# A two-layer attention, scan and expert step on one core: longer runs for the gate and up weights, and a first norm taken tile by tile

## What is computed

```
def adaln(x, g, shift, scale):
    return rms_norm(x, g) * (1 + scale) + shift        # eps 1e-6 inside the root

# attention, layer 0: per head
q = rms_norm(q.reshape(b, t, 16, 64), q_g); k = rms_norm(k.reshape(b, t, 4, 64), k_g)

# experts, after each mixer (t: 640 x 1024)
scores = sigmoid(t @ router_w)                         # 1024 x 16, shared by both layers
...                                                    # one group of 4, then 2 experts in it
hg = einsum('td,edf->tef', t, w_gate)                  # w_gate, w_up: 16 x 1024 x 256
hu = einsum('td,edf->tef', t, w_up)
out = einsum('tef,efd->td', silu(hg) * hu * gates, w_down)   # w_down: 16 x 256 x 1024
```

## Time and profile before

| | |
|---|---|
| runs | 1648.84, 1651.23, 1654.79 us |
| the profiled execution's own time | 1647.64 us |
| its span, first to last instruction | 1645.7 us |
| PE busy | 1452.9 us, 88% of the span |
| DVE, ACT, POOL busy | 581.2, 560.2, 177.6 us |
| bytes moved | 323.25 MB, mean 196 GB/s |
| gate, up, down loads | 40 each, 1 MB each, 20 per layer |

### The profile page before, as it was taken

One profiled execution on the slowest core, in us unless ns is written; L12 is line 12 of the kernel. 1 busy time (PEld: TensorE's weight loads), 2 busy tenths in 40 slices (PEclk: granted clock), 3 DMA queues, 4 the chain that ended last, 5 costly groups with the idle time before them and its releaser, 6 DMA issues.

```text
span 1645.7 us, 18690 instructions
## 1 busy us (share of the span) xinstructions
PE 1452.9 (88%) x7371; PEld 727.6 (44%) x7371; DVE 581.2 (35%) x927; ACT 560.2 (34%) x1228; POOL 177.6 (11%) x177
## 2 busy tenths in 40 slices
PE   5998799999969998488899899899889997899970
PEld 3444454444443333165455455455454444433320
DVE  1133556662450000173545545545452033300004
ACT  4112444441112221253573573573570011122211
POOL 0122000000010000200310400400410100200002
PEclk9999999999979999769999999999999999899985
DMA  9502666469289999633133133133054123999985
GB/s 346 207 1 94 227 198 227 158 206 360 89 307 345 380 379 380 246 107 119 58 121 103 64 116 102 65 114 103 26 187 184 43 73 111 362 368 381 384 311 204
DMA packets 193889, 323.25 MB, mean 196 GB/s; under 512 B 8822, under 2 KB 120006, under 8 KB 193798
## 3 DMA queue, kind: packets, MB, share of 16 engines
q1 hardware_dynamic: 172956, 260.33, 46.5%
q0 software_dynamic: 8496, 31.17, 5.0%
q10 hardware_dynamic: 12352, 30.58, 4.7%
HBM read 279.05 MB, written 42.99 MB: 196 GB/s over the span
## 4 chain that ended last, share of the span: by engine, by line
PE 76%; DVE 9%; DMA 6%; ACT 4%; issue 3%; SPq 2%; POOL 0%; ACTq 0%; DVEq 0%; POOLq 0%
PE ps L945 10%; PE ps L1041 10%; PE ps L1201 8%; PE ps L1096 8%; PE ps L732 7%; PE ps L966 5%; PE ps L895 4%; PE ps L679 3%; PE ps L1043 2%; PE ps L822 2%; PE ps L806 2%; DMA mem<-in_expert_w_up 2%; PE ps L1180 2%; PE ps L929 1%; PE ps L1172 1%
## 5 line engine op out<-in xcount | busy, mean ns | idle before, releaser
L945 PE MATMUL ps<-mem 128*32 128x512 f32 (+1 forms) x1408 | 204.2, 606 | 9.3 <-DMA mem<-in_expert_w_up 7.2
L1041 PE MATMUL ps<-mem 128*128 128x512 f32 x384 | 171.2, 599 | 0.2 <-ACT mem L1566 0.2
L1201 PE MATMUL ps<-mem 128*128 128x512 f32 x320 | 139.0, 593 | 3.2 <-issue 2.7
L1096 PE MATMUL ps<-mem 128*128 128x512 f32 x320 | 140.7, 593 | 0.3 <-ACT mem L1566 0.3
L1891 DVE TENSOR_TENSOR mem<-ps,mem 128x256 f32<-128x256 f32 x28 | 11.9, 425 | 362.1 <-ACT mem L1386 362.1
L1961 DVE SCALAR_TENSOR_TENSOR mem<-mem 128x642 f32<-128x642 f32 x96 | 92.6, 965 | 87.5 <-ACT mem L1490 85.0
L945 PEld LDWEIGHTS ps<-mem 128*32 128x32 f32 (+1 forms) x1408 | 60.3, 119 | 136.5 <-issue 134.0
L966 PE MATMUL ps<-mem 128*32 128x512 f32 (+1 forms) x704 | 106.5, 609 | 11.8 <-DMA mem<-in_expert_w_down 8.0
L732 PE MATMUL ps<-mem 128*128 128x512 f32 x240 | 109.2, 613 | 1.9 <-DVE mem L1665 1.9
L1041 PEld LDWEIGHTS ps<-mem 128*128 128x128 f32 x384 | 72.0, 192 | 82.3 <-issue 81.5
L1526 ACT ACTIVATE mem<-mem,small 128x128 f32<-128x128 f32 x320 | 95.2, 392 | 25.4 <-DMA mem<-cum_rows 25.4
(11 more groups left out here) (315 smaller groups left out, 1944.5 us busy)
## 6 DMA issues: line engine op xcount, KB each, us to landing
mem<-in_mod_w SPq DMA_DIRECT2D x24, 2048.0 KB, 8.6
mem<-in_expert_w_gate SPq DMA_DIRECT2D x40, 1024.0 KB, 12.5
mem<-in_expert_w_up SPq DMA_DIRECT2D x40, 1024.0 KB, 14.1
mem<-in_expert_w_down SPq DMA_DIRECT2D x40, 1024.0 KB, 12.9
mem<-cum_rows SPq DMA_DIRECT2D x40, 512.0 KB, 5.3
slot_rows<-mem ACTq DMA_DIRECT2D x28, 512.0 KB, 7.0
mem<-slot_rows ACTq DMA_DIRECT2D x26, 512.0 KB, 8.1
slot_rows<-mem SPq DMA_DIRECT2D x1, 12288.0 KB, 53.6
```

The source lines that it names most:

```text
L945: last = nc.tensor.matmul(ps[c:c + w, 2 + j, :], XGT[j][:, k, c:c + w], GUW[l][m][:, k, :], start=(k == 0), stop=(k == KD - 1))
L1041: nc.tensor.matmul(ps[:, b, :], w[:, k, :], HT[:, k, SEQ:TOK], start=(k == 0), stop=(k == KD - 1))
L1096: last = nc.tensor.matmul(ps[:, ZBANK[t], :], HT[:, k, t * P:(t + 1) * P], WZ[2 * k // KD][:, k % (KD // 2), :], start=(k == 0), stop=(k = ...
L1201: last = nc.tensor.matmul(ps[:, 4 + n % 4, :], YT[b][:, k, t * P:(t + 1) * P], w[:, k, :], start=(b == 0 and k == 0), stop=(b == 1 and k = ...
```

## The change

Four edits, in one program.

1. **Gate and up weights.** Both are read as `e (p k) f`: partition p holds the rows 8p to 8p+7, which lie together in memory, one run of 2048 floats (8 KB) for each partition and transfer. The tile becomes `[p, 2, k, f]`: all of gate, then all of up. The product takes `GUW[l][m][:, :, k, :]`, two pieces of 256 columns. Since row 8q+k of the weights is now on partition q of step k, the tokens' columns are permuted in the same way: `norm_row` writes its first result into the scratch `JUNK`, and the addition of the shift writes element `8q+k` to column `128k+q` of `H`. The router's weights are loaded in the same order. The down weights are as before.
2. **First norm.** `X` comes as three transfers on three semaphores (context tile; latent tiles 1 and 2; tiles 3 and 4). ACT takes square and root of each tile in turn, with the copies of turned tiles between them, and takes one root of a dummy before, which loads the function table. DVE takes a reciprocal and scales, tile by tile. PE turns all five tiles ahead of `early_chunk(0)`.
3. **Head norm.** The multiplication by 1/64 and the addition of eps move into ACT's root.
4. Semaphores are shared between uses to stay within their number; a wait on `s_h` guards `JUNK` in `norm_row` (from the second tile on) and in the attention's residual.

```diff
-        GUW = [[page(at, 4 * PG).rearrange("p (k n) -> p k n", k=KD) for at in order] for order in (...)]
+        GUW = [[page(at, 4 * PG).rearrange("p (a k n) -> p a k n", a=2, k=KD) for at in order] for order in (...)]
...
-            sp.dma_start(X[:, 0, :], x_prompt[0]).then_inc(s_x, 16)
-            sp.dma_start(X[:, 1:NT, :], x_sample[0].rearrange("(t p) n -> p t n", p=P)).then_inc(s_x, 16)
+            sp.dma_start(X[:, 0, :], x_prompt[0]).then_inc(s_xy, 16)
+            sp.dma_start(X[:, 1:3, :], xv[:, 0:2]).then_inc(s_rows, 16)
+            sp.dma_start(X[:, 3:NT, :], xv[:, 2:NT - 1]).then_inc(s_x, 16)
...
-            sp.dma_start(RW[:, 0:KD, :], router_w.rearrange("(k p) e -> p k e", p=P)).then_inc(s_x, 16)
+            sp.dma_start(RW[:, 0:KD, :], router_w.rearrange("(p k) e -> p k e", p=P)).then_inc(s_x, 16)
...
-                gv = w_gate[l].rearrange("e (k p) f -> e p k f", p=P)
-                uv = w_up[l].rearrange("e (k p) f -> e p k f", p=P)
+                gv = w_gate[l].rearrange("e (p k) f -> e p (k f)", p=P)
+                uv = w_up[l].rearrange("e (p k) f -> e p (k f)", p=P)
...
-                    sp.dma_start(GUW[l][m][:, :, 0:FF], gv[e]).then_inc(pk["lgu"][m], 16)
-                    sp.dma_start(GUW[l][m][:, :, FF:2 * FF], uv[e]).then_inc(pk["lgu"][m], 16)
+                    sp.dma_start(GUW[l][m][:, 0].rearrange("p k f -> p (k f)"), gv[e]).then_inc(pk["lgu"][m], 16)
+                    sp.dma_start(GUW[l][m][:, 1].rearrange("p k f -> p (k f)"), uv[e]).then_inc(pk["lgu"][m], 16)
...
-            early_chunk(0)
             norm_transposes(0)
+            early_chunk(0)
             early_chunk(1)
...
-                            last = nc.tensor.matmul(ps[c:c + w, 2 + j, :], XGT[j][:, k, c:c + w], GUW[l][m][:, k, :],
+                            last = nc.tensor.matmul(ps[c:c + w, 2 + j, :], XGT[j][:, k, c:c + w], GUW[l][m][:, :, k, :],
...
+            order(nc.scalar.activation(ssq[:, 5:6], eps[:, :], ACT.Sqrt))
+            for t in range(NT + 2):
+                if t < NT:
+                    row_lengths(t)
+                if t >= 2:
+                    norm_columns(t - 2)
...
-                nc.scalar.activation(rs[:, :], rs[:, :], ACT.Sqrt).then_inc(s_sdq, 1)
+                nc.scalar.activation(rs[:, :], rs[:, :], ACT.Sqrt, scale=1.0 / HD, bias=eps[:, :]).then_inc(s_sdq, 1)
...
-                order(nc.vector.scalar_tensor_tensor(H[:, t, :], X[:, t, :], ssq[:, t:t + 1], MB[1][:, 1, min(t, 1), :],
+                if t >= 1:
+                    dve.wait_ge(s_h, nn * NT + t)
+                order(nc.vector.scalar_tensor_tensor(JUNK, X[:, t, :], ssq[:, t:t + 1], MB[1][:, 1, min(t, 1), :],
                                                      op0=ALU.mult, op1=ALU.mult))
-                nc.vector.tensor_tensor(H[:, t, :], H[:, t, :], MB[1][:, 0, min(t, 1), :], ALU.add).then_inc(s_h, 1)
+                nc.vector.tensor_tensor(H[:, t, :].rearrange("p (k q) -> p q k", k=KD), JUNK.rearrange("p (q k) -> p q k", k=KD),
+                                        MB[1][:, 0, min(t, 1), :].rearrange("p (q k) -> p q k", k=KD), ALU.add).then_inc(s_h, 1)
...
-                nc.vector.tensor_scalar(rs[:, :], rs[:, :], 1.0 / HD, EPS, ALU.mult, ALU.add).then_inc(s_varq, 1)
```

More of the change, by code:

```diff
@@ L230, in backbone @@
         HELD = [len(range(m, NE, RING)) for m in range(RING)]
-        GUW = [[page(at, 4 * PG).rearrange("p (k n) -> p k n", k=KD) for at in order] for order in ((18, 22, 10, 14, 28), (22, 10, 18, 14, 28))]
+        GUW = [[page(at, 4 * PG).rearrange("p (a k n) -> p a k n", a=2, k=KD) for at in order] for order in ((18, 22, 10, 14, 28), (22, 10, 18, 14, 28))]
         WD = [page(at, 2 * D).rearrange("p (k n) -> p k n", k=2) for at in (26, 5, 7, 36, 34)]
@@ L310, in backbone @@
         s_gqk = sem("s_gqk")
-        s_qkv, s_sq, s_v, s_varq, s_sdq, s_qn, s_qg, s_t2, s_qf, s_tq, s_tqe = (
-            sem(n) for n in "s_qkv s_sq s_v s_varq s_sdq s_qn s_qg s_t2 s_qf s_tq s_tqe".split())
+        s_qkv, s_sq, s_v, s_rsq, s_sdq, s_qn, s_qg, s_t2, s_qf, s_tq, s_tqe = (
+            sem(n) for n in "s_qkv s_sq s_v s_rsq s_sdq s_qn s_qg s_t2 s_qf s_tq s_tqe".split())
         s_S, s_Sc, s_max, s_exp, s_T, s_ptd, s_pta, s_pv, s_oev, s_rx, s_rs, s_Scc = (
@@ L316, in backbone @@
         o_u, o_cv, o_pv, o_y = sem("o_u"), sem("o_cv"), sem("o_pv"), sem("o_y")
-        s_zero, s_clear = sem("s_zero"), sem("s_clear")
+        s_zero, s_rows = sem("s_zero"), sem("s_rows")
         s_ssdin, s_pre_pe, s_pre_act, s_pre_dve = (sem(n) for n in "s_ssdin s_pre_pe s_pre_act s_pre_dve".split())
@@ L595, in _ @@
                 sp.wait_ge(ES["x2"], NT + t + 1)
-                sp.dma_start(y_prompt[0] if t == 0 else y_sample[0, (t - 1) * P:t * P, :], X[:, t, :]).then_inc(s_yout, 16)
+                sp.dma_start(y_prompt[0] if t == 0 else y_sample[0, (t - 1) * P:t * P, :], X[:, t, :]).then_inc(s_xy, 16)
         @block.tensor
@@ L629, in logit_columns @@
                 if t == 0:
-                    pe.wait_ge(s_x, 64)
+                    pe.wait_ge(s_x, 48)
                     if l == 0:
@@ L708, in early_chunk @@
                 mod_chunk(EX[n % 2], n, 7, s_exused[n % 2])
+            norm_transposes(0)
             early_chunk(0)
-            norm_transposes(0)
             early_chunk(1)
@@ L1228, in _, with row_lengths, norm_columns @@
             order = Order(act, o_act)
[L1230 to L1243, removed]
+            def row_lengths(t):
+                if t <= 1:
+                    act.wait_ge((s_xy, s_rows)[t], 16)
+                elif t == 3:
+                    act.wait_ge(s_x, 16)
+                order(nc.scalar.activation(SQX, X[:, t, :], ACT.Square, accum_out=ssq[:, t:t + 1]))
+                nc.scalar.activation(ssq[:, t:t + 1], ssq[:, t:t + 1], ACT.Sqrt, scale=1.0 / D, bias=eps[:, :]).then_inc(s_sd, 1)
+            def norm_columns(t):
+                act.wait_ge(s_ht, t + 1)
+                nc.scalar.activation(HT[:, :, t * P:(t + 1) * P],
+                                     psf[:, (t % 2) * 1024:(t % 2) * 1024 + 1024].rearrange("p (k n) -> p k n", k=KD),
+                                     ACT.Copy).then_inc(s_hT, 1)
             def modulate(h):
@@ L1616, in logit_columns, with first_norm @@
                 nc.vector.tensor_copy(LT[:, n % 2, :], ps[:, 3, 2 * P:3 * P]).then_inc(s_ltc, 1)
-            def norm_plain(nn):
-                dve.wait_ge(s_sd, nn + 1)
-                order(nc.vector.reciprocal(ssq[:, 0:NT], ssq[:, 0:NT]))
+            def first_norm():
                 for t in range(NT):
+                    dve.wait_ge(s_sd, t + 1)
+                    order(nc.vector.reciprocal(ssq[:, t:t + 1], ssq[:, t:t + 1]))
                     nc.vector.tensor_scalar(H[:, t, :], X[:, t, :], ssq[:, t:t + 1], None, ALU.mult).then_inc(s_h, 1)
@@ L1667, in modulate @@
                     last.then_inc(s_apd, 1)
-            dve.wait_ge(s_x, 32)
-            norm_plain(0)
+            first_norm()
             dve.wait_ge(s_partc, 1)
@@ L1788, in _ @@
                 b = 2048 + 1024 * (t % 2)
+                if t >= 1:
+                    dve.wait_ge(s_h, NT + t)
                 nc.vector.tensor_tensor(JUNK, psf[:, b:b + D], MB[0][:, 2, min(t, 1), :], ALU.mult).then_inc(s_opm, 1)
@@ L1798, in moe @@
                 dve.wait_ge(ES["score"], l + 1)
-                dve.wait_ge(s_x, 64)
+                dve.wait_ge(s_x, 48)
                 order(V_.tensor_tensor(biased, score, RB[:, :].unsqueeze(1).to_broadcast([P, NT, NE]), ALU.add))
@@ L1907, in scaled @@
                 def scaled(t):
-                    dve.wait_ge(s_sd, 1 + NT + t + 1)
+                    dve.wait_ge(s_sd, 2 * NT + t + 1)
                     order(V_.reciprocal(ssq[:, t:t + 1], ssq[:, t:t + 1]))
@@ L2162, in moe @@
                 if l == 0:
-                    pool.wait_ge(s_clear, 16)
+                    pool.wait_ge(s_rows, 32)
                 for t in range(NT):
@@ L2226, in _ @@
             pool.wait_ge(s_out, 32)
-            pool.wait_ge(s_yout, 16 * NT)
+            pool.wait_ge(s_xy, 16 * (NT + 1))
 _INS = ["x_prompt", "x_sample", "c", "c_ctx", "cache_k", "cache_v", "state_ssm", "mod_w", "mod_b", "norm1_g",
```

13 lines of the change are left out of this document (6 added, 7 removed).

## The result

The changed kernel takes 1643.92 us in the median of 11 runs, the kernel before 1651.67 in 13 beside it. The ratio of the two is 0.995 (95% interval 0.9927 to 0.9974), so 4 to 12 us were gained where 25 were forecast, and the median is 6 us above the range. Two slow executions of the changed kernel (1690.88 and 3831.48 us), and one of `before_busy` further down (2584.4), are left out of all medians, spreads and ratios. The profiled execution took 1636.22 us and is one of the two shortest. That last point is not harmless: this trace lies 8 us under the median of its series, and 10 under that of the next series of the same kernel (1646.75), so both traces had to be read by stages.

What follows compares the result with a forecast made beforehand. Expert stages were taken as bound by weight transfers, the debt paid at their end, on a chain 76% TensorE. Opening -3.9, head norm -0.2, stages -10.5 and -10.8, write +0.6: -24.8 us, from 1651.2 to 1626.4; range 1618 to 1638.

Steps and rivals of the forecast that it cites:

- Edit 1's supply: Expert stages: gate and up loads in 8 KB runs go at 408 GB/s instead of 348, saving 0.89 us an expert.
- both hold, by 3 and 1 us: Layer 0's surplus packs: first down weights land by 650.7, needed at 653.6; last up weights by 656.2, needed at 657.3.
- Edit 1's price on the path: End of the expert stages: the surplus packs finish 10.5 us sooner in layer 0 and 10.8 us in layer 1.
- without waits: Surplus packs at full clock with no wait on PE: 26.2 us, layer 0 ending at 670.4 instead of 680.8.
- the rows of the packs come too late: Rival, mild form: row loads pace base packs at 12.9 us, losing 10 us that surplus packs win back; 1648 us, chance 0.08.
- if the surplus packs still wait: Sign in the expert stages' ends that the prediction is wrong; it expected no DMA wait over 1 us at PE there.
- Edit 2: Opening: first norm tile by tile lets PE's second chunk start at its landing, 22.5, and QKV near 29.4; 3.9 us gained.
- Edit 3: Head norm: one DVE instruction leaves the chain, where it stands once, for the last tile; 0.2 us gained.
- The permuted write: Norm ahead of the experts: the addition's irregular write costs 0.3 us more a layer, 0.6 in all.
- the doubling of the rival: Rival: each permuted word takes two turns, the addition 2.5 us, costing 2.5 in all instead of 0.6; 1628 us, chance 0.16.
- no faster: Rival: 8 KB runs of gate and up weights move no faster than 1 KB; 3.5 us gained, 1648 us, chance 0.08.
- strongly late: Rival: the packs' row loads land so late that packs take 14 us each; 1670 us, slower, chance 0.06.

Runs made afterwards that it cites:

- before_busy: The kernel before plus constant products keeping TensorE at work in the gap between first expert stage and scan: 1651.23 us, ratio 0.9984.
- the pair with busy products: The kernel before and the changed kernel, each with constant products added between first expert stage and scan: 1651.23 and 1643.85 us, 7.4 us apart.
- both_first: The changed kernel with both surplus packs' gate and up products ahead of the first one's turn and down product: 1641.18 us, ratio 0.9914.

## Why the prediction was wrong, step by step

**Edit 1's supply: right.** 408 GB/s was forecast, 407 and 424 came. No weight is waited for in the surplus packs, as "both hold, by 3 and 1 us" said. The two stages of the versions without the rows' wait are 11.0 and 10.8 us shorter than before (the table's means), against 10.5 and 10.8 in the sum. Part of this closeness is luck: the surplus packs, for which the sum stood, gave 9.5 and 10.1, and the base packs, which it left out, the rest.

**Edit 1's price on the path: wrong, and this is the step that failed.** The changed kernel got 4.7 and 3.7 us of these (the table again), and only 2.0 and 2.3 of them in the surplus packs; the others are base packs that end sooner. The prediction took "the base packs end", added a pack's instructions "without waits" and asked of the supply of weights alone whether it was early enough. Its list of what a pack does named the turn of rows only inside "a step of turns and copies 2.4". It weighed the rows' load for the base packs, which "is used two packs later, so 12 us of landing are free", and did not ask the same of the loop, where the load is issued with the first surplus pack and wanted one product later, 4.5 us (640.90 to 645.4). A landing of 9.5 us stood in the rows of before, and the order of the calls in the code. Beside the longer runs the rows' loads also land later: 11.0 to 11.3 us in the median in the ten profiles with edit 1, 8.1 to 8.3 in the four without. The base packs did not suffer from it: where row loads are issued two packs ahead, no wait was shown. What the runs showed in place of "without waits" is a wait of 4.7 and 5.3 us for rows and a half clock behind it; with the wait gone, and most of the half clock with it, the surplus packs end 7.5 and 7.8 us sooner (the table). So "the rows of the packs come too late" was the right transfer and the wrong place: the rival priced a slower cadence of base packs. That its 1648 is close to the measured time is luck, since it took the loss from the base packs and gave the surplus packs their gain. The prediction's own sign, "if the surplus packs still wait", did come.

**Edit 2: right in its mechanism, mis-sized.** The second chunk started at its landing, 22.44 (forecast 22.5), the QKV product at 28.8 (forecast 29.4) in three of the eight changed openings and at 29.03 in a fourth. In the other four it started at 30.8 to 31.8, since the clock was halved from 23 or 24 us on, ahead of the product (the second chunk took 2.57 to 3.49 us in place of 1.93). At attention's end 2.2 us of the 4.1 (edits 2 and 3 together) are left on average, with single profiles from 379.9 to 386.0. The kernel before had its half clock behind the chunks, between 30 and 40 us (0.73 and 0.59 granted in the two halves), and the five profiles without edits 2 and 3 stand within 1.2 us.

**Edit 3:** the multiplication is gone from the chain; the root with its scale and bias takes 0.32 where ACT's plain root took 0.23 before. Its own gain is not told apart in any run.

**The permuted write: mis-sized, over the dearest row.** 1.91 us a tile against 1.24, +0.67 and not +0.3, on the chain once in each layer: 1.3 us. It isn't the doubling of the rival either (2.5 us). A page of the Trainium skill that the rival named, *Vector Engine (DVE) Microarchitecture Reference*, Measured stream behaviour on trn2, has 1.7 to 2.5 ns a column for such writes; 1.91 us over 1024 columns is 1.87, and the trace agrees. The nearest row wasn't near.

**The sum as it came:** stages 8.4 and opening 2.2 gained, 1.3 paid, 9.3 us in all. The two ratios of the changed kernel give 8.3 and 7.1, the pair with busy products 7.4. The prediction had 24.8: 12.9 of the difference are the stages (the rows' wait and the clock behind it cost more, the base packs gave some back), 1.9 the opening, 0.7 the write.

**The other cases.** The 358 GB/s that the prediction quoted from the Trainium skill (*DMA: Bandwidth & Descriptors*, Bandwidth) do not bind here: 407 over 120 us, 424 over 4. The same section says that this is each core's part when both cores of a pair stream; here one core ran, which the prediction overlooked. Neither "no faster" nor "strongly late" happened.

**What stays open:** why the clock falls in one execution at a place where it doesn't in the next. The runs of one version spread over 4 us (`both_first`, 6 runs) to 21 us (the changed kernel, 12 runs), with and without each edit; they don't show what sets the clock off. Whether the rows' load could have been issued sooner, in place of being waited for later, wasn't tried. Nor was 8 KB against 4 KB: that the length of the runs sets the rate rests on gate and up loads of 1 and 8 KB alone.

## What to carry to other kernels

When a late transfer is sped up, write down every wait that PE meets in the stage behind it, with its issue time and its landing, those for other data too; the next one in the order of the code decides, not the sum of busy times. A wait for data that a later iteration needs belongs behind this iteration's work, where it costs nothing (here the order of a few calls was worth 12 to 16 us, but only once the weights were on time). And compare stages over several profiles: a single trace here lies up to 9 us from the median of its own series, and the granted clock differs with it.

## What the runs showed of the hardware

- Gate and up loads with 8 KB to a partition moved at 424 GB/s, those of 1 KB at 348; the 512 KB loads of rows beside them landed 3 us later than before, 11.1 against 8.1, the stores 1 us, 8.1 against 7.0.
- The fp32 addition that writes 1024 columns 512 bytes apart took 1.91 us, in ten instances between 1.89 and 1.95; in order it took 1.24 (1.22 by the instruction itself).
- Filling a 19 us gap of PE kept the granted clock at 1.00 in it (0.56 without), but the clock fell at other places afterwards (0.86 from 720 to 730 us), and the program was 0.16% faster, within its uncertainty.
